# The last attention branch of a four-layer model: its input split in two halves, its first two weight chunks side by side, and gates by tanh

## The chip, the cores and the metric

The kernel runs on one core of one Trainium2 chip. The metric is device time in microseconds (us) of one execution of the whole program; lower is better.

## What is computed

Four transformer layers over 256 tokens of width 1024, in fp32. Layers 0 and 1 have a delta rule, a pooling and a retention as mixers; layers 2 and 3, which the change is mostly about, have three kinds of attention (`a` with a top-64 choice of keys, `b` dilated, `c` windowed with sinks). Each layer gates three branch products and sums them:

```python
g = jax.nn.sigmoid(gates.reshape(Bsz, L, N_BRANCHES, D_MODEL))
merged = (g[:, :, 0] * (o_a.reshape(Bsz, L, -1) @ w_a)
          + g[:, :, 1] * (o_b.reshape(Bsz, L, -1) @ w_b)
          + g[:, :, 2] * (o_c.reshape(Bsz, L, -1) @ w_c))
return merged @ w_o
```

`w_a` has 384 rows, `w_b` 256 and `w_c` 512; all have 1024 columns. After `w_o` comes a norm and a feed-forward block (`w_up`, squared relu, `w_down`). Layers 0 and 1 gate three branches in the same way.

## The kernel before

Everything is kept transposed: 128 features on the partitions, the 256 tokens along the free axis. A weight matrix comes as chunks of 128 x 1024 elements (eight 128 x 128 tiles, 512 KB) through four raw buffers. fp32 accuracy is made of two rounded parts: for each chunk ScalarE (ACT) copies `raw` to the high part `whi` and VectorE (DVE) makes the low part `wlo = raw - whi` (every second chunk or so of the second half is made by GpSimd, POOL, instead: `SHARED`, L155 on). Both go to rings of four buffers. An input of a product is split in the same way (`hh`/`hl`, `B0H`/`B0L`, `B2H`/`B2L`, `FH`/`FL`). Each tile of a product then is three matmuls (`mm3`, L1867), so a chunk is 24 matmuls on TensorE (PE).

All engines walk the same list of jobs, each in its own program order, and wait for each other by semaphores. While a chunk `i` is multiplied, ACT and DVE split chunk `i + 3` (`STAGED`); that split must wait until PE has used chunk `i - 1` up (the signal `used`). In layers 2 and 3 the attention's small steps are interleaved with a filler of weight products: `run(attention(...), fill)`, with the filler q2b (16 chunks), gate0 (8), gate1 (8), wa (3), gate2 (8), wb (2). The attention has ten rounds, numbered by `turn` 0 to 9; each round passes through five segments (scores, exponentials, turning the probabilities, values, output turned back to `OO`), and the rounds overlap. Rounds 6 to 9 are kind `c` and make wc's input, the four blocks 5 to 8 of `OO`: rounds 6 and 8 write blocks 5 and 6 for the first and the second half of the tokens, rounds 7 and 9 blocks 7 and 8. So the first half of wc's input is complete after round 8, the second after round 9. When the ten rounds are over, one filler step is left: the second chunk of wb. After that comes wc, then wo.

At the end of attention the program order is: ACT copies the output of round 9 to `OO`, makes `B2H` (`branch_high`, L780), then in the filler splits the chunk of wb's last step, and at wc's begin computes two sigmoids of 128 x 1024 in place (`branch`, L790). DVE makes `B2L` (`branch_low`, L1271), then splits a chunk, then evacuates the last two banks of wb: `evac` (L1282) multiplies a bank of two product tiles by the gate. The products of wb, wc, gate0 to gate2 alternate between two PSUM banks, 6 and 7; PE's `fresh` (L1856) waits until the previous contents of a bank were evacuated. POOL adds the gated products to `YY`. In wc, `merge` (L813 on ACT, L1302 on DVE) splits the sum `YY` to `FH` and `FL`, the input of wo, by quarters.

ScalarE's function tables: `act` (L614) loads the set `natural_log_exp_and_others` by hand ahead of an Exp or Ln when another function's set was in use last (L611 in the profile); ahead of a Sigmoid the load is put in by the compiler (L618). In the norm ahead of the feed-forward (`factor`, L652) an Ln and an Exp follow PE's sum, and the products of `up` can't be evacuated before them.

Of the kernel before, what the change touches and what calls it, by code (L numbers as in the profile page):

```python
# [25 lines left out]
EXPLN = "natural_log_exp_and_others"  # L26

# [173 lines left out]
def rest(steps):  # L201
    for _ in steps:
        pass
# [61 lines left out]
def program(nc, ins, out):  # L265
    with ExitStack() as ctx:
# [111 lines left out]
        BR2 = slot_r("B2H", 11, 4), slot_r("B2L", 13, 4)  # L378
# [226 lines left out]
        def scalar(a):  # L605
            table = [None]

            def ln_exp():
                if table[0] != EXPLN:
                    table[0] = EXPLN  # L610
                    a.preload_act_table_set(EXPLN)  # L611

            def act(dst, src, fn, scale=1.0, **more):
                if fn in (AF.Exp, AF.Ln):  # L614
                    ln_exp()
                elif fn in (AF.Silu, AF.Sigmoid, AF.Sin):
                    table[0] = str(fn)
                return a.activation(dst, src, fn, scale=scale, **more)  # L618
# [170 lines left out]

            def branch(name, L, merged=False):  # L790
                gate, dst = BRANCH[name][2:]

                def begin():
                    for j in (0, 2):
                        a.wait_ge(*v_evac.at(gate, L, 2 * j + 2))
                        d = dst[:, 512 * j:512 * j + 1024]
                        act(d, d, AF.Sigmoid).then_inc(*a_br.up("gate", name, L, j))

                begin()
# [13 lines left out]
            def merge(name, L, j):  # L813

                a.wait_ge(*gated(name, L, 2 * j))
                a.copy(FH[:, 2 * j:2 * j + 2, :], v3(pair(YY, j))).then_inc(*a_br.up("sum", L, j))
# [99 lines left out]
            def second(L):  # L916
# [29 lines left out]

                def index(half):
# [13 lines left out]
                def attend(x):  # L961
# [11 lines left out]
                    for q, (b, c0, heads) in enumerate(x.spread):  # L973
# [4 lines left out]
                        else:  # L978
                            p = a.copy(PT[:, c0:c0 + m], bank[b][:, 0:m])
                        p.then_inc(*a_att.up("PT", L, t, q))  # L980
                    yield
# [4 lines left out]

                fill = chain(project("q2b", L), project("gate0", L),
                             after_step(project("gate1", L), 5, lambda: branch_high("wa", L, *a_att.at("OO", L, 1))),
                             branch("wa", L),
                             after_step(project("gate2", L), 5, lambda: wb_high()),  # L990
                             branch("wb", L))
# [6 lines left out]
                branch_high("wc", L, *a_att.at("OO", L, 9))  # L998
                rest(fill)
                rest(branch("wc", L, merged=True))  # L1000

# [52 lines left out]
        def vector(v):  # L1054
# [224 lines left out]
            def branch(name, L, merged=False):  # L1279
                gate = BRANCH[name][3]  # L1280

                def evac(m0):  # L1282
# [4 lines left out]
                    if name in FIRST_BRANCH:  # L1287
                        tt(YY[:, c], b[:, :], gate[:, c], OP.mult).then_inc(*v_evac.up(name, L, m0))
                        return
                    tt(gate[:, c], b[:, :], gate[:, c], OP.mult).then_inc(*v_evac.up(name, L, m0))  # L1290
# [1284 lines left out]
```

## Time and profile before

| | us |
|---|---|
| median of 3 runs | 1928.36 (1928.3 to 1932.68) |
| the profiled execution, its own time | 1935.99 |
| span of its trace | 1934.2 |
| PE busy | 1887.0 (98% of the span) |
| DVE busy | 1238.2 (64%) |
| ACT busy | 958.4 (50%) |
| POOL busy | 311.4 (16%) |

A busy PE need not be at its peak, so the places are found by the idle time in front of an instruction and what ended it. Layers 2 and 3 repeat each other 449.5 us apart, and layer 2 is read except where said. Times in rows are us from the start of the span unless marked ns.

### The profile page before, as it was taken

How to read it: one execution, taken by the hardware profiler on the slowest of the kernel's cores; microseconds unless marked ns; L12 is line 12 of the kernel's file. 1: busy time of each engine (PE TensorE's matmuls, PEld its weight loads, DVE VectorE, ACT ScalarE, POOL GpSimd, SP SyncE). 2: the span in 40 equal slices, each digit the busy share in tenths (PEclk: the TensorE clock that was granted, in tenths of full speed). 3: DMA queues.
4: the chain of work that ended last, by engine and by line, in shares of the span. 5: the costliest groups of instructions: out<-in, count | busy, mean ns of one | idle time of the engine just before them, and what ended most of it. 6: DMA issues, size and time to landing. Idle time of an engine off the chain costs nothing.

```text
span 1934.2 us, 35101 instructions
## 1 busy us (share of the span) xinstructions
PE 1887.0 (98%) x14820; PEld 1800.6 (93%) x14820; DVE 1238.2 (64%) x1667; ACT 958.4 (50%) x1375; POOL 311.4 (16%) x174
## 2 busy tenths in 40 slices
PE   7999999999999999999999999999999999999998
PEld 7989998998889999999988999999999999999997
DVE  6884577665579545867657775577646684567743
ACT  5533365544563344654445445655534444656632
POOL 1050121000014102200001352310000353220000
PEclk9999999999999999999999999999999999999999
DMA  5443344656344323545665553345555763345652
GB/s 209 158 138 108 121 161 140 215 196 205 134 142 159 115 99 127 201 164 186 196 206 176 178 190 121 132 153 198 188 186 172 219 191 123 131 161 176 197 196 99
DMA packets 91580, 317.50 MB, mean 164 GB/s; under 512 B 11552, under 2 KB 12704, under 8 KB 91040
## 3 DMA queue, kind: packets, MB, share of 16 engines
q1 hardware_dynamic: 91424, 315.26, 48.7%
q8 instruction: 118, 1.93, 0.4%
q14 instruction: 38, 0.31, 0.0%
HBM read 304.99 MB, written 1.05 MB: 158 GB/s over the span
## 4 chain that ended last, share of the span: by engine, by line
PE 83%; DVE 12%; ACT 4%; issue 1%; DMA 0%; SPq 0%; ACTq 0%; DVEq 0%
PE bank L1863 81%; DVE wlo L1056 4%; DVE area L1056 3%; DVE area L1062 2%; ACT area L618 1%; ACT whi L624 1%; PE bank L2302 1%; PE bank L2042 1%; DVE xT L1062 0%; DMA raw<-in_weights 0%; DVE hl L1062 0%; DVE area L1527 0%; ACT hh L618 0%; DVE area L1525 0%; PE bank L2320 0%
## 5 line engine op out<-in xcount | busy, mean ns | idle before, releaser
L1056 DVE TENSOR_TENSOR wlo<-raw,whi 128x1024 fp32r<-128x1024 f32 x512 | 657.0, 1296 | 427.6 <-ACT whi L624 427.2
L1863 PE MATMUL bank<-hh,whi 128*128 128x256 f32 x2928 | 834.0, 285 | 26.4 <-DVE wlo L1056 18.7
L1863 PE MATMUL bank<-hl,whi 128*128 128x256 f32 x2928 | 817.6, 279 | 0.0
L1863 PE MATMUL bank<-hh,wlo 128*128 128x256 f32 x2928 | 817.4, 279 | 0.0
L624 ACT CAST whi<-raw 128x1024 fp32r<-128x1024 f32 x572 | 588.2, 1046 | 398.5 <-PE bank L1863 368.5
L1863 PEld LDWEIGHTS bank<-hh,whi 128*128 128x128 f32 x2928 | 556.9, 190 | 41.8 <-issue 15.1
L1863 PEld LDWEIGHTS bank<-hl,whi 128*128 128x128 f32 x2928 | 556.0, 190 | 1.5 <-issue 1.4
L1863 PEld LDWEIGHTS bank<-hh,wlo 128*128 128x128 f32 x2928 | 555.7, 190 | 0.0
L1655 POOL TENSOR_TENSOR area<-area 128x512 f32<-128x512 f32 (+4 forms) x90 | 138.3, 1544 | 929.8 <-ACT area L618 675.9
L1655 POOL TENSOR_TENSOR wlo<-raw,whi 128x1024 fp32r<-128x1024 f32 x60 | 151.5, 2526 | 332.1 <-ACT whi L624 331.7
L1863 PE MATMUL bank<-area 128*128 128x128 f32 (+5 forms) x1544 | 200.3, 289 | 4.1 <-DVE area L1056 3.3
L1863 PEld LDWEIGHTS bank<-area 128*128 128x128 f32 (+2 forms) x1544 | 181.2, 188 | 18.4 <-DVE area L1056 4.6
L1863 PE MATMUL bank<-FH,whi 128*128 128x256 f32 x640 | 178.6, 279 | 0.0
L1863 PE MATMUL bank<-FL,whi 128*128 128x256 f32 x640 | 178.3, 279 | 0.0
L1863 PE MATMUL bank<-FH,wlo 128*128 128x256 f32 x640 | 178.2, 279 | 0.0
L618 ACT ACTIVATE area<-area 128x256 f32<-128x256 f32 (+9 forms) x247 | 140.0, 578 | 60.3 <-DVE area L1056 20.7
L1056 DVE TENSOR_TENSOR area<-bank,area 128x512 f32<-128x512 f32 (+4 forms) x194 | 116.6, 629 | 57.1 <-PE bank L1863 52.9
L1863 PEld LDWEIGHTS bank<-FH,whi 128*128 128x128 f32 x640 | 121.5, 190 | 0.1
L1863 PEld LDWEIGHTS bank<-FL,whi 128*128 128x128 f32 x640 | 120.1, 188 | 0.1
L1863 PEld LDWEIGHTS bank<-FH,wlo 128*128 128x128 f32 x640 | 120.1, 188 | 0.0
L1056 DVE TENSOR_TENSOR area<-bank,RSB 128x512 f32<-128x512 f32 (+1 forms) x118 | 80.4, 682 | 51.4 <-PE bank L1863 51.4
L1863 PE MATMUL bank<-wlo,FH 128*128 128x512 f32 x240 | 94.6, 394 | 0.0
(123 smaller groups left out, 1883.6 us busy)
## 6 DMA issues: line engine op xcount, KB each, us to landing
raw<-in_weights SPq DMA_DIRECT2D x572, 512.0 KB, 3.7
area<-area SPq DMA_DIRECT2D x96, 64.0 KB, 3.7
area<-area SPq DMA_DIRECT2D x16, 128.0 KB, 3.8
cst<-in_const SPq DMA_DIRECT2D x1, 1188.0 KB, 10.1
cst<-in_const SPq DMA_DIRECT2D x1, 1024.5 KB, 5.6
xT<-in_x SPq DMA_DIRECT2D x4, 256.0 KB, 5.8
out<-xT SPq DMA_DIRECT2D x1, 1024.0 KB, 3.8
area<-in_lev SPq DMA_DIRECT2D x2, 384.0 KB, 7.7
```

Of the source, the lines that this page charges most:

```text
L618: return a.activation(dst, src, fn, scale=scale, **more)
L624: a.copy(whi[:, i % RING, :], raw[:, i % RAW, :]).then_inc(*hi.up(i))
L1056: return v.tensor_tensor(dst, x, y, op)
L1062: return v.scalar_tensor_tensor(out=dst, in0=x, scalar=s, in1=y, op0=op0, op1=op1)
L1655: return g.tensor_tensor(dst, x, y, op)
L1863: return e.matmul(ps, x, y, start=start, stop=stop, skip_group_check=skip)
L2042: x = e.transpose(bank[b0 + j][:, 128 * (b % 4):128 * (b % 4) + 128], block(src, b), C("eye"))
L2302: o = e.transpose(bank[b][:, 128 * u:128 * u + 128], x.grid()[:, j % 2, j // 2, 128 * kb:128 * kb + 128], C("eye"))
```

## The change

Chunks of wc are called F, F+1, F+2 and F+3; wo's are F+4 to F+11.

- `B2H` and `B2L` move from slots that the attention uses to its end to slots 3 and 4 (query and key blocks of kind `b`, free by then). Their 128 x 1024 split becomes two of 128 x 512: `wc_high(0)` and `wc_low(0)` in round 9's third segment, `wc_high(1)` and `wc_low(1)` after the attention.
- PE runs wc by `last_branch`: it waits for chunks F and F+1 and for both banks, multiplies the first half of the input with both chunks, then the second half, then F+2 and F+3 one after the other.
- Sigmoid(x) becomes (tanh(x/2) + 1)/2: ACT computes the tanh, DVE's `evac` adds 1 and multiplies (`scalar_tensor_tensor` in place of `tensor_tensor`), and `merge` multiplies by 0.5. This holds for all four layers.
- In layers 2 and 3 the set `exp_and_others` (Exp and Tanh) is loaded once ahead of attention and the logarithm's set after wc's merges; the gates are computed in the filler: wa's after steps 1 and 3 of gate1, wb's after steps 0 and 1 of wa, wc's after steps 0 and 1 of wb. As a step's follow-up runs when the filler is next called, wc's first gate stands after `wc_high(1)` and ahead of the split of chunk F+2, and its second behind that split.

```diff
-        BR2 = slot_r("B2H", 11, 4), slot_r("B2L", 13, 4)
+        BR2 = slot_r("B2H", 3, 4), slot_r("B2L", 4, 4)
@@ scalar
-                if fn in (AF.Exp, AF.Ln):
+                if fn is AF.Tanh:
+                    tables(EXPTANH)
+                elif fn is AF.Ln or fn is AF.Exp and table[0] != EXPTANH:
                     ln_exp()
...
+            def gate(name, L, j):
+                projection, dst = BRANCH[name][2:]
+                a.wait_ge(*v_evac.at(projection, L, 2 * j + 2))
+                d = dst[:, 512 * j:512 * j + 1024]
+                act(d, d, AF.Tanh, scale=0.5).then_inc(*a_br.up("gate", name, L, j))
...
-                a.copy(FH[:, 2 * j:2 * j + 2, :], v3(pair(YY, j))).then_inc(*a_br.up("sum", L, j))
+                act(FH[:, 2 * j:2 * j + 2, :], v3(pair(YY, j)), AF.Copy, scale=0.5).then_inc(*a_br.up("sum", L, j))
...
                 rest(project("v2b", L, v_second))
+                tables(EXPTANH)
+                def wc_high(j):
+                    a.wait_ge(*a_att.at("OO", L, 8 + j))
+                    a.copy(BR2[0][:, 2 * j:2 * j + 2, :], v3(BRANCH["wc"][1])[:, 2 * j:2 * j + 2, :]).then_inc(*a_br.up("high", "wc", L, j))
...
+                def gates(name, steps, *at):
+                    for i, s in enumerate(steps):
+                        yield s
+                        if i in at:
+                            gate(name, L, 2 * at.index(i))
                 fill = chain(project("q2b", L), project("gate0", L),
-                             after_step(project("gate1", L), 5, lambda: branch_high("wa", L, *a_att.at("OO", L, 1))),
-                             branch("wa", L),
+                             gates("wa", after_step(project("gate1", L), 5, lambda: branch_high("wa", L, *a_att.at("OO", L, 1))), 1, 3),
+                             gates("wb", branch("wa", L), 0, 1),
                              after_step(project("gate2", L), 5, lambda: wb_high()),
-                             branch("wb", L))
+                             gates("wc", branch("wb", L), 0, 1))
...
                 run(attention(index, attend), fill)
-                branch_high("wc", L, *a_att.at("OO", L, 9))
+                wc_high(1)
                 rest(fill)
                 rest(branch("wc", L, merged=True))
+                ln_exp()
@@ vector
-                    tt(gate[:, c], b[:, :], gate[:, c], OP.mult).then_inc(*v_evac.up(name, L, m0))
+                    stt(gate[:, c], gate[:, c], 1.0, b[:, :], OP.add, OP.mult).then_inc(*v_evac.up(name, L, m0))
...
-                tt(FL[:, 2 * j:2 * j + 2, :], v3(pair(YY, j)), FH[:, 2 * j:2 * j + 2, :].bitcast(F32), OP.subtract).then_inc(*v_br.up("merged", L, j))
+                stt(FL[:, 2 * j:2 * j + 2, :], v3(pair(YY, j)), 0.5, FH[:, 2 * j:2 * j + 2, :].bitcast(F32), OP.mult, OP.subtract).then_inc(*v_br.up("merged", L, j))
...
                 run(attention(index, attend), fill)
-                branch_low("wc", L)
+                wc_low(1)
@@ tensor
+            def last_branch(L):
+                job = JOBS["wc", L]
+                h, lo = BR2
+                for c in (0, 1):
+                    e.wait_ge(*wlo_at(job.first + c))
+                    fresh(job.banks[2 * c], leaves("wc", L, 2 * c))
+                for j in range(2):
+                    e.wait_ge(*v_br.at("low", "wc", L, j))
+                    for m in range(4):
+                        i, b = job.first + m // 2, job.banks[m // 2 * 2]
+                        for k in (2 * j, 2 * j + 1):
+                            x = mm3(bank[b][:, T * (m % 2):T * (m % 2) + T], i, 128 * (4 * (m % 2) + k), h[:, k, :], lo[:, k, :], (m % 2, k) == (0, 0), k == 3, True)
+                        if j and m % 2:
+                            x.then_inc(*proj.up("used", i, also=("wc", L, m - 1)))
+                for c in (2, 3):
+                    ...
-                rest(branch("wc", L))
+                last_branch(L)
```

## Rows read from the trace of the kernel before

**Rows 1.** PE's waits over the whole run: released by, total us, times, longest.
```profile
PE bank L1863 <- DVE wlo L1056: 18.7, 11, 11.3
PE bank L1863 <- DVE area L1056: 9.9, 9, 2.4
```
**Rows 2.** Timeline of PE, start, us, what [idle before]: wb's chunks and wc's begin.
```profile
1254.69 0.35 PE L1863 MATMUL bank<-B0H,whi 128*128 128x256 f32 x1 [0.30 <-DVE area L1056]
...
1260.09 0.35 PE L1863 MATMUL bank<-B2H,whi 128*128 128x256 f32 x1 [2.34 <-DVE area L1056]
```
**Rows 3.** Timeline of DVE over the same stretch and into wc.
```profile
1252.71 1.23 DVE L1056 TENSOR_TENSOR wlo<-raw,whi 128x1024 fp32r<-128x1024 f32 x1 [0.96 <-ACT whi L624]
...
1255.92 2.33 DVE L1056 TENSOR_TENSOR B2L<-area,B2H 128x1024 fp32r<-128x1024 f32 x1 [0.78 <-ACT B2H L788]
1258.17 1.21 DVE L1056 TENSOR_TENSOR wlo<-raw,whi 128x1024 fp32r<-128x1024 f32 x1
1259.31 1.27 DVE L1056 TENSOR_TENSOR area<-bank,area 128x512 f32<-128x512 f32 x2
...
1263.26 0.69 DVE L1056 TENSOR_TENSOR area<-bank,area 128x512 f32<-128x512 f32 x1 [0.23 <-PE bank L1863]
```
**Rows 4.** Timeline of ACT, end of attention and wo's weight splits.
```profile
1248.45 1.28 ACT L618 ACT_TABLE_LOAD   x1
...
1251.65 1.03 ACT L624 CAST whi<-raw 128x1024 fp32r<-128x1024 f32 x1
1254.43 0.37 ACT L984 COPY area<-bank 128x256 f32<-128x256 f32 x1 [1.74 <-PE bank L2320]
1254.83 1.06 ACT L788 CAST B2H<-area 128x1024 fp32r<-128x1024 f32 x1
1255.78 1.05 ACT L624 CAST whi<-raw 128x1024 fp32r<-128x1024 f32 x1
1256.74 2.00 ACT L618 ACTIVATE area<-area 128x1024 f32<-128x1024 f32 x2
...
1283.03 1.05 ACT L624 CAST whi<-raw 128x1024 fp32r<-128x1024 f32 x1 [1.78 <-PE bank L1863]
```
**Rows 5.** Timeline of POOL: the adds of wb's first two banks.
```profile
1254.62 2.54 POOL L1655 TENSOR_TENSOR area<-area 128x512 f32<-128x512 f32 x2 [3.73 <-DVE area L1056]
```
**Rows 6.** Layer 3: wc's begin on PE, its evacuation, the last merge, the split behind it.
```profile
1709.60 0.55 PE L1863 MATMUL bank<-B2H,whi 128*128 128x256 f32 x1 [2.44 <-DVE area L1056]
...
1714.19 0.69 DVE L1056 TENSOR_TENSOR area<-bank,area 128x512 f32<-128x512 f32 x1 [1.66 <-PE bank L1863]
...
1726.08 2.95 ACT L624 CAST whi<-raw 128x1024 fp32r<-128x1024 f32 x3
...
1727.16 1.23 DVE L1056 TENSOR_TENSOR wlo<-raw,whi 128x1024 fp32r<-128x1024 f32 x1 [0.26 <-ACT whi L624]
```
**Rows 7.** Windows: us, PE busy (matmuls), granted clock, DMA share, GB/s.
```profile
1709.40:1712.80 3.40, 3.20 (x15) 0.50 0.45 154
```
**Rows 8.** Timeline of ACT and PE: the norm ahead of the feed-forward's products.
```profile
1301.65 1.28 ACT L611 ACT_TABLE_LOAD   x1 [2.75 <-PE bank L1863]
1302.95 0.48 ACT L618 ACTIVATE RSB<-bank,cst 128x256 f32<-128x256 f32 x1
...
1307.58 0.38 PE L1863 MATMUL bank<-hh,whi 128*128 128x256 f32 x1 [0.50 <-DVE wlo L1056]
```
**Rows 9.** Timeline of ACT, then DVE, as attention begins.
```profile
1082.88 0.60 ACT L618 ACTIVATE area<-bank 128x512 f32<-128x512 f32 x1 [0.29 <-PE bank L1863]
...
1094.93 1.29 DVE L1056 TENSOR_TENSOR area<-bank,area 128x512 f32<-128x512 f32 x2 [0.94 <-PE bank L1863]
```
**Rows 10.** Groups by form: count, busy us, mean ns, idle before.
```profile
L1056 DVE TENSOR_TENSOR area<-bank,area 128x512 f32<-128x512 f32 x156 | 102.1, 683 | 22.9 <-PE bank L1863 19.1 <-PE bank L2042 3.4
L1062 DVE SCALAR_TENSOR_TENSOR area<-bank,area 128x512 f32<-128x512 f32 x4 | 2.6, 680 | 0.0
L788 ACT CAST B0H<-area 128x512 fp32r<-128x512 f32 x2 | 1.2, 608 | 0.0
```

More of the change, by code:

```diff
@@ L606, in scalar, with tables @@
             table = [None]
+            def tables(which):
+                if table[0] != which:
+                    table[0] = which
+                    a.preload_act_table_set(which)
             def ln_exp():
-                if table[0] != EXPLN:
-                    table[0] = EXPLN
-                    a.preload_act_table_set(EXPLN)
+                tables(EXPLN)
             def act(dst, src, fn, scale=1.0, **more):
-                if fn in (AF.Exp, AF.Ln):
+                if fn is AF.Tanh:
+                    tables(EXPTANH)
+                elif fn is AF.Ln or fn is AF.Exp and table[0] != EXPTANH:
                     ln_exp()
-                elif fn in (AF.Silu, AF.Sigmoid, AF.Sin):
+                elif fn in (AF.Silu, AF.Sin):
                     table[0] = str(fn)
@@ L788, in branch_high @@
                 a.copy(BRANCH[name][0][0][:, 0:nk, :].rearrange("p k t -> p (k t)"), BRANCH[name][1]).then_inc(*a_br.up("high", name, L))
-            def branch(name, L, merged=False):
[L791 to L799, printed above, removed]
+            def gate(name, L, j):
[3 more added lines that the diff above has]
+                act(d, d, AF.Tanh, scale=0.5).then_inc(*a_br.up("gate", name, L, j))
+            def branch(name, L, merged=False):
+                if L < DEPTH:
+                    gate(name, L, 0)
+                    gate(name, L, 2)
                 if not merged:
@@ L980, in attend @@
                         p.then_inc(*a_att.up("PT", L, t, q))
+                    if t == 9:
+                        wc_high(0)
                     yield
@@ L1287, in evac @@
                     if name in FIRST_BRANCH:
[L1288 removed]
+                        stt(YY[:, c], gate[:, c], 1.0, b[:, :], OP.add, OP.mult).then_inc(*v_evac.up(name, L, m0))
                         return
[L1290 removed]
+                    stt(gate[:, c], gate[:, c], 1.0, b[:, :], OP.add, OP.mult).then_inc(*v_evac.up(name, L, m0))
                     if m0 == 6:
@@ L1569, in attend @@
                     v.reciprocal(x.den, x.den).then_inc(*v_att.up("den", L, t))
+                    if t == 9:
+                        wc_low(0)
                     yield
@@ L1580, in attend, with wc_low @@
                     yield
+                def wc_low(j):
+                    v.wait_ge(*a_br.at("high", "wc", L, j))
+                    at = slice(2 * j, 2 * j + 2)
+                    tt(BR2[1][:, at, :], v3(BRANCH["wc"][1])[:, at, :], BR2[0][:, at, :].bitcast(F32), OP.subtract).then_inc(*v_br.up("low", "wc", L, j))
                 def gate2(m0):
@@ L2216, in branch @@
                 yield from project(name, L, h, lo, lambda j: v_br.at("low", name, L))
+            def last_branch(L):
[13 more added lines that the diff above has]
+                for c in (2, 3):
+                    i, b = job.first + c, job.banks[2 * c]
+                    e.wait_ge(*wlo_at(i))
+                    fresh(b, leaves("wc", L, 2 * c))
+                    for m in range(2):
+                        for k in range(4):
+                            x = mm3(bank[b][:, T * m:T * m + T], i, 128 * (4 * m + k), h[:, k, :], lo[:, k, :], k == 0, k == 3)
+                    x.then_inc(*proj.up("used", i, also=("wc", L, 2 * c)))
             def first(L):
```

1 line of the change is left out of this document (added).

## The prediction

> **What bounds the kernel now.** TensorE (PE) is busy for 98% of the span, so time is won or lost only where PE stands still or runs slower. I read PE's waits of the whole run first [rows 1]: the long ones are for weight splits early in the run and for VectorE's (DVE) results; 9.9 us in nine waits, the longest 2.4, are for DVE's work on `area`. Two of those nine are the places that the change aims at. The timeline shows the place in layer 2 [rows 2]: PE waits 0.30 us ahead of wb's second chunk, finishes it at 1257.75 (that is 1260.09 less 2.34) and begins wc at 1260.09. Layer 3 has the same picture, 2.44 us long [rows 6]. A third stop follows in the norm ahead of `up`, 0.50 us [rows 8]; I take the same in layer 3. If all of it went, 2 x (0.30 + 0.50) + 2.34 + 2.44 = 6.4 us would be won, 0.33% of the run. That is the ceiling of what waits are worth here.
>
> Then I asked which chain ends the 2.3 us. `B2H` begins 0.03 us after ACT's last output copy (1254.43 + 0.37 = 1254.80) and takes 1.06 [rows 4]; `B2L` takes 2.33, since it runs beside POOL's two adds [rows 3, 5]. But PE doesn't begin when `B2L` is there (1258.25). DVE next splits the chunk F+2 (1.21 us), and only then evacuates wb's last two banks, 1259.31 on, 0.60 from one to the next; PE's 1260.09 is the end of the first of these (1260.00) plus 0.09 [rows 2, 3]. So the wait ends with a bank that DVE frees behind two other works in its queue. The split F+2 in turn can't start before ACT's copy of F+2, 1255.78 to 1256.83 [rows 4], which is early today and hidden behind `B2L`.
>
> **The change, part by part.** (1) The first half of `B2H`/`B2L`. Round 8's output is copied a round earlier, and ACT gets 3.2 us free, as the load and two sigmoids leave (the load starts at 1248.45, and the next split at 1251.65 [rows 4]). A 128 x 512 copy costs 0.61 on ACT [rows 10] and DVE's half half of 1.22, the time of an undisturbed 128 x 1024 split [rows 3]; both are covered by PE's chunk of gate2. Cost nothing. If that cover were gone they would cost 1.2 us a layer.
>
> (2) wb's second chunk. The load and the sigmoids (3.2 us) leave ACT ahead of the split F+1, so DVE does this split before 1252.7 and not from 1252.71 on [rows 3, 4], and frees wb's first bank as soon as PE has filled it. PE's 0.30 goes; wb ends at 1257.45.
>
> (3) The start of wc, the main term. What is late next? ACT, counted by the distance from one start to the next [rows 4]: output copy ends 1254.80; `wc_high(1)` starts 1254.83 and, at half of 0.95, gives way at 1255.35 (0.52, with the fixed part); the new first gate, a tanh of 128 x 1024, which I price as the sigmoid (2.00 for two, so about 0.95 a piece), 1256.30; the split of F+2 ends 1.05 later, 1257.35. `wc_low(1)` is done by then, even if it waits for POOL's adds to end: those follow wb's evacuations and end at about 1256.1. DVE splits F+2 from 1257.38 (1.14 to the next start), evacuates the first bank from 1258.52 and the second from 1259.12 to 1259.80. And `last_branch` waits for both banks before its first matmul, not for one as now. PE begins at 1259.80 + 0.09 = 1259.89, against 1260.09: 0.20 us won of 2.3. The gate that was moved ahead of the split takes what the halved split gives. Bounds: nothing (the tanh longer by 0.2) to 2.64 (the wait goes wholly); the chain of rows is complete, so I stay at 0.20.
>
> (4) Side by side. Work on PE is the same 96 matmuls, 2.83 us a chunk (ACT's split of 1283.03 sits 1.05 long with 1.78 idle before it, paced by PE [rows 4]). But the first chunk is given back after 36 matmuls and not 24: 4.25 us after wc's start, plus the 0.34 that lies between that and DVE's evacuation today (1263.26 - 1260.09 - 2.83). Layer 3 shows by chance what that does downstream: there its first chunk ran at a half clock, and DVE's evacuation began 1714.19 - 1709.60 = 4.59 us after wc's start [rows 6]. So I read the rest of the branch there. No stall of PE followed within wc. The split of wo's fourth chunk, F+7, started on DVE at 17.56 after wc's start, behind all four merges. PE will want that chunk (4 + 3) x 2.83 = 19.81 after the start. Today it has 1.0 us to spare.
>
> (5) The tables. In layers 2 and 3 four loads (1.28 each) become two. The one that leaves the norm is on the path: PE's sum, load, Ln, Exp, DVE, split, PE [rows 8]; the chain gets 1.28 shorter and PE's 0.50 goes, no more. The one that is put behind the merges stands on ACT ahead of the split of F+7: 17.56 + 1.28 + 1.23 = 20.07, plus 0.09 is 20.16, so PE stops 0.35 us. Bounds of that: zero, to 1.44 if one more collision with POOL (2.33 - 1.22 = 1.1 [rows 3]) gets into the chain of merges. I take 0.35, the row's. The load as attention begins delays two small works by about half a us [rows 9]; DVE has 0.94 idle further down before PE needs it. Nothing. Loads and sigmoids inside attention: PE doesn't wait there, nothing.
>
> (6) DVE's adds of 1 and the scalings: `scalar_tensor_tensor` with a bank takes 0.680, `tensor_tensor` 0.683 [rows 10]. Nothing, in all four layers. In layers 0 and 1 the number of loads stays, as a logarithm follows.
>
> The Trainium skill ("ScalarE: Activation LUTs", What ACT_TABLE_LOAD costs) says that a switch costs a drain of about 1380 ns beside the 1283 ns of the load. The trace speaks against a visible drain: the Ln begins 1.30 us after the load's start [rows 8]. By the page's figure the stop in wo would be an estimated 1.7 us and the sum 2.1 us slower; I go by the row.
>
> **Sum.** Per layer -0.20 + 0.35 - 0.50 = -0.35, so -0.7 for both. The profiled execution would go from 1935.99 (span 1934.2 and 1.8 around it) to 1935.3. It is 7.6 above the median of the runs, and none of the terms depends on what lies between them, so I carry the difference over: 1928.36 - 0.7 = 1927.7.
>
> **The rivals.** *The clock.* In layer 3 the granted clock fell to 0.50 (1.2 GHz) right where the idle stretch ended, for 3.4 us [rows 7]; the first evacuation came 4.59 - 3.17 = 1.42 us later than in layer 2. In layer 2 a wait 0.1 shorter had no such fall. After the change PE's idle stretch is 2.44 (1257.45 to 1259.89), and 2.54 in layer 3: as long as now. So the fall may go (1927.7 - 1.4 = 1926.3), stay, or come in both layers (1929.1). Nothing in the rows tells which; 18% and 17%.
>
> *The gap closes wholly.* If PE found both banks free and the halves ready, layer 2 would win 2.64 + 0.50 - 0.35 = 2.8, layer 3 2.9 and its 1.42 of clock: 7.1, so 1921.3. For it: the low half is what the wait seems to be for. Against it: the bank is, and ACT's order. 6%.
>
> *wo's fourth chunk comes late (slower).* The place is PE's fourth chunk of wo; the mechanism is the ring: chunks given back 1.4 us later, merges behind them, the table load behind these, then the split. It decides from the point where DVE ends that split later than 19.8 us after wc's start. At 1.44 a layer: -0.20 + 1.44 - 0.50 = +0.74, twice 1.5: 1929.9. For it: only 1.0 us to spare with 1.28 put in. Against: layer 3's rows have most of it in already. 8%.
>
> *The change doesn't do what it says.* If the set with Exp doesn't serve the tanh (or the reverse), the compiler puts loads in again, one of 1.28 in ACT's chain of (3): +1.28 a layer, 1928.36 - 0.7 + 2.6 = 1930.2. For: Sigmoid needed its own load at L618 until now. Against: Ln and Exp share one. 5%.
>
> **How the numbers follow.** Forecast 46%, clock gone 18%, clock in both 17%, late chunk 8%, gap closed 6%, loads 5%. The likeliest is 1927.7. The range 1924.0 to 1931.0 leaves out the closed gap and a late chunk or loads that meet the clock, and holds a part-closed gap. About 0.3%, 5.8 us, is what a measurement of this kernel can tell from no change: below 1922.6 lies the closed gap (6%), above 1934.1 only mishaps that add up (3%).
>
> **What would show it.** Right: in the trace of after PE's wait ahead of wc is 2.3 to 2.7 us and ends with DVE's second evacuation of wb; the split of F+2 starts on ACT at about 1.5 us after the output copy's end, behind a tanh; the 0.30 and the 0.50 are gone; a short stop appears at wo's fourth chunk, released by `wlo`. Wrong: a wait ahead of wc under 1 us; a stop inside wc (a bank not freed by its second evacuation); any load between Exp and tanh; new waits of PE within attention.

## The result and the profile after

| | before | after |
|---|---|---|
| median, us (20 runs of each, taken together) | 1934.42 (1926.9 to 1938.17) | 1938.9 (1930.4 to 1948.5) |
| profiled execution, us (its span) | 1935.99 (1934.2) | 1942.33 (1940.5) |
| ratio, with its 95% interval | | 1.0029 [1.0016, 1.0042] |

The forecast was 1927.7, with 1924.0 to 1931.0: that is 0.7 us faster. The kernel became slower by 4.5 us (difference of the medians) to 5.6 (the ratio). So the sign was wrong, though the size is just under the 0.3% that I called "same". Some 6 us of the distance between 1927.7 and 1938.9 are no effect of the change: the kernel before itself came out at 1934.42 here, against 1928.36 in its three first runs. That fact turned out to be a clue. One profiled execution, that of bank_and_order_2, ran at a granted clock of 0.85 from end to end (2083.5 us, where its series otherwise lies between 1920.52 and 1941.04), and neither its time nor its trace is used.

The page of after, busy time of each engine:
```profile
PE 1891.2 (97%) x14820; PEld 1804.8 (93%) x14820; DVE 1245.0 (64%) x1669; ACT 952.8 (49%) x1373; POOL 307.8 (16%) x174
```
PE's waits over the whole run of after, released by, total us, times, longest; to be laid beside [rows 1]:
```profile
PE bank L1895 <- DVE wlo L1080: 18.6, 11, 11.3
PE bank L1895 <- DVE area L1080: 6.2, 6, 1.9
PE bank L1895 <- DVE area L1086: 5.9, 2, 2.9
```
The timeline of PE in after: a matmul ahead of wb's second chunk, wc's first, and wo's fourth chunk, in layer 2; then the last two places in layer 3.
```profile
1254.91 0.28 PE L1895 MATMUL bank<-B0H,wlo 128*128 128x256 f32 x1
...
1261.43 0.35 PE L1895 MATMUL bank<-B2H,whi 128*128 128x256 f32 x1 [2.93 <-DVE area L1086]
...
1283.27 0.36 PE L1895 MATMUL bank<-FH,whi 128*128 128x256 f32 x1 [0.75 <-DVE wlo L1080]
...
1715.01 0.36 PE L1895 MATMUL bank<-B2H,whi 128*128 128x256 f32 x1 [2.93 <-DVE area L1086]
...
1736.85 0.36 PE L1895 MATMUL bank<-FH,whi 128*128 128x256 f32 x1 [0.34 <-DVE wlo L1080]
```
Against [rows 2, 6 and 8]: the 0.30 ahead of wb's second chunk is gone (no bracket around 1254.91), so is the norm's 0.50; the wait ahead of wc is 2.93 in both layers instead of 2.34 and 2.44; and wo's fourth chunk has a stop of its own. Below I count a stop from the start of the last matmul before it to the first one behind it, where two matmuls without a stop lie 0.12 apart.

ACT and DVE of after as wb ends, and as wo begins (to be laid beside [rows 3 and 4]):
```profile
1255.80 0.37 ACT L1000 COPY area<-bank 128x256 f32<-128x256 f32 x1 [3.73 <-PE bank L2376]
1256.20 0.62 ACT L959 CAST B2H<-area 128x512 fp32r<-128x512 f32 x1
1256.73 1.06 ACT L624 ACTIVATE area<-area 128x1024 f32<-128x1024 f32 x1
1257.69 1.03 ACT L630 CAST whi<-raw 128x1024 fp32r<-128x1024 f32 x1
...
1279.51 1.28 ACT L612 ACT_TABLE_LOAD   x1
1280.81 3.90 ACT L630 CAST whi<-raw 128x1024 fp32r<-128x1024 f32 x4
```
```profile
1256.86 1.34 DVE L1080 TENSOR_TENSOR B2L<-area,B2H 128x512 fp32r<-128x512 f32 x1 [0.59 <-ACT B2H L959]
1258.76 1.23 DVE L1080 TENSOR_TENSOR wlo<-raw,whi 128x1024 fp32r<-128x1024 f32 x1 [0.56 <-ACT whi L630]
1259.90 1.28 DVE L1086 SCALAR_TENSOR_TENSOR area<-area,bank 128x512 f32<-128x512 f32 x2
...
1281.89 4.63 DVE L1080 TENSOR_TENSOR wlo<-raw,whi 128x1024 fp32r<-128x1024 f32 x4 [1.68 <-ACT whi L630]
```
Windows of PE behind wc's start in after: us, PE busy (matmuls), granted clock, DMA share, GB/s:
```profile
1262.40:1265.70 3.30, 3.30 (x17) 0.50 0.37 129
1716.40:1719.70 3.30, 3.30 (x18) 0.50 0.41 146
```
Before, only layer 3 had such a stretch at 0.50 (1.2 GHz) [rows 7]; in after both layers have it.

**What these places add up to.** wb's stop and the start of wc together: the output copy begins at 1255.80 and wc 5.63 later, against 5.66 before (1260.09 - 1254.43): nothing. The norm's two stops, 0.77 and 0.78, are 0.12 now: -1.3. wo's fourth chunk, 1.02 and 0.61 instead of 0.12: +1.4. One more stretch at half clock: +1.4. The sum is +1.5. The two profiled executions differ by 6.3. Another 1.6 is one stop in layer 3, as attention begins, which the second trace of the same kernel (below) doesn't have:
```profile
1583.14 0.36 PE L1895 MATMUL bank<-hh,whi 128*128 128x256 f32 x1 [1.45 <-DVE area L1080]
```
That leaves 3.2 us without a stop of that size, and 2.4 of them lie between matmuls that don't wait at all.

### The profile page after: what moved, and what is told of

Its sections match the earlier page's. It is cut to its first block, busy times and chain, and to the rows that moved or that the text cites. A ratio compares the mean times of both kernels' runs of the same rounds, so it can differ in the third digit from the quotient of the medians.

```text
span 1940.5 us, 35101 instructions
## 1 busy us (share of the span) xinstructions
PE 1891.2 (97%) x14820; PEld 1804.8 (93%) x14820; DVE 1245.0 (64%) x1669; ACT 952.8 (49%) x1373; POOL 307.8 (16%) x174
## 4 chain that ended last, share of the span: by engine, by line
PE 82%; DVE 13%; ACT 4%; issue 2%; DMA 0%; SPq 0%; DVEq 0%; ACTq 0%
PE bank L1895 80%; DVE wlo L1080 5%; DVE area L1080 3%; DVE area L1086 2%; ACT area L624 2%; ACT whi L630 1%; PE bank L2358 1%; PE bank L2074 1%; DVE xT L1086 0%; DVE area L1551 0%; DVE area L1549 0%; DVE area L1083 0%; DVE hl L1086 0%; DMA raw<-in_weights 0%; ACT hh L624 0%
## 5 line engine op out<-in xcount | busy, mean ns | idle before, releaser
L624 ACT ACTIVATE area<-area 128x256 f32<-128x256 f32 (+8 forms) x247 | 140.7, 579 | 61.0 <-DVE area L1080 21.0
L1080 DVE TENSOR_TENSOR area<-bank,area 128x512 f32<-128x512 f32 (+4 forms) x146 | 84.1, 610 | 44.9 <-PE bank L1895 41.2
```

The lines of the kernel that those rows point to most:

```text
L1080: return v.tensor_tensor(dst, x, y, op)
```

## PE runs at one of two paces

I laid the 14,820 matmuls of both traces side by side, by number. Away from stops, at full granted clock, the distance between two matmuls of 128 x 256 isn't one number. It is 113.3 ns or 117.8 ns, hardly anything between, and it holds for hundreds of matmuls, in the long stretches for more than a thousand. In the 19 traces at full clock that this study has, it never changes within 96 or more matmuls that follow each other without a break. The kernel after passes from one to the other inside the norm of layer 2; its PE timeline there, wo's last matmuls, the sum with ones, then `up`:
```profile
1302.10 0.28 PE L1895 MATMUL bank<-hl,whi 128*128 128x256 f32 x1
1302.22 0.28 PE L1895 MATMUL bank<-hh,wlo 128*128 128x256 f32 x1
1302.33 0.28 PE L1895 MATMUL bank<-hh,whi 128*128 128x256 f32 x1
1302.44 0.28 PE L1895 MATMUL bank<-hl,whi 128*128 128x256 f32 x1
1302.56 0.28 PE L1895 MATMUL bank<-hh,wlo 128*128 128x256 f32 x1
1302.67 1.89 PE L1895 MATMUL bank<-area,cst 128*128 128x256 f32 x8
1304.21 0.47 PE L1895 MATMUL bank<-hh,whi 128*128 128x256 f32 x1
1304.51 0.28 PE L1895 MATMUL bank<-hl,whi 128*128 128x256 f32 x1
1304.63 0.28 PE L1895 MATMUL bank<-hh,wlo 128*128 128x256 f32 x1
1304.75 0.28 PE L1895 MATMUL bank<-hh,whi 128*128 128x256 f32 x1
1304.87 0.28 PE L1895 MATMUL bank<-hl,whi 128*128 128x256 f32 x1
1304.99 0.28 PE L1895 MATMUL bank<-hh,wlo 128*128 128x256 f32 x1
```
Four steps take 0.46 us above (1302.10 to 1302.56) and 0.48 below (1304.51 to 1304.99). A window of 50 us holds about 443 matmuls at the short distance and 427 at the long one. The same two windows, first in layer 2 and then in layer 3, for before and then for after and for a second profile of the same kernel (after_again); columns as above:
```profile
1380.00:1430.00 50.00, 50.00 (x427) 1.00 0.57 190
1830.00:1880.00 50.00, 50.00 (x443) 1.00 0.59 198
```
```profile
1380.00:1430.00 50.00, 50.00 (x427) 1.00 0.59 187
1830.00:1880.00 50.00, 50.00 (x444) 1.00 0.64 197
```
```profile
1380.00:1430.00 50.00, 50.00 (x427) 1.00 0.60 190
1830.00:1880.00 50.00, 50.00 (x427) 1.00 0.60 189
```
PE is busy all the time and the clock is 1.00 in all six: the page's share of busy time can't show this, only the count can. One kernel has it either way in different executions. The some 1450 matmuls of `up` and `down` behind a norm take 1450 x 4.5 ns = 6.5 us more at the long distance, over four times what all the places add up to. The first traces of before and after have the same pace in both windows, so the 2.4 us of pace between those two lie outside `up` and `down`. The same program's executions spread over 11 us here (1926.9 to 1938.17; over all series of the kernel before 1926.54 to 1950.82), and in the traces that follow the pace goes a long way with that: the three with the short pace in both layers have spans of 1923.6 to 1932.0, the eight with the long one in both 1933.2 to 1942.7. It isn't all: before_again, with the paces of before in both windows, has a span 4.7 us shorter, and about 5 us less of stops and half clock in layers 0 and 1.

## The experiments

Ratios are to the kernel before, run beside it on the same chip, 12 runs of each experiment; the brackets are 95% intervals. First the kernel after once more, and three undoings. "The rest" below is the mean difference to before minus what stops and half-clock stretches in the trace give; I work it out for all kernels further down.

**after_again.** Nothing edited.

> The changed kernel as it is, to learn what repeats. Theory 'places' (the loss sits where PE stops: 2.93 us ahead of wc in both layers, a clock at 1.2 GHz behind it, 0.9 and 0.5 us at wo's fourth chunk, 1.45 us as attention begins in layer 3): these stops stand at the same instructions again, and the ratio to the kernel before is 1.002 to 1.004. Rival 'pace' (in the two traces PE needs either 2.72 or 2.83 us for 24 matmuls without any wait, and the stretches of either differ; that makes 2.8 of the 6.3 us between the traces): the stretches lie elsewhere in this trace, though the kernel is the same, and the stop as attention begins in layer 3 may be gone.

1.0031 [1.0008, 1.0053], 1941.84 us. Same stops (3.21 at wc in both layers, 1.02 at wo in both), the half clock in one layer only, and the long pace in both layers. The slowdown is real, and which stretches are at which pace changes from one execution to the next. In the profile of after the 1.45 us stop as attention begins in layer 3 looked like an effect of the change; it isn't here, so it was chance. A stop of that length comes elsewhere too, in layer 2 of before_no_stop_3 (1.73 us between starts), a kernel without the change.

**no_side.** The last branch in the project order, chunk by chunk.
```diff
-                last_branch(L)
+                h, lo = BR2
+                rest(project("wc", L, h, lo, lambda j: v_br.at("low", "wc", L, j)))
```


> The changed kernel, with wc's chunks one after the other on PE as before (the input still split in halves, one bank waited for). Theory 'the second bank and the two chunks held': PE begins wc after the first evacuation, 0.6 us sooner, and gives the first chunk back 1.4 us sooner, so the stop at wo's fourth chunk goes (0.9 and 0.5 us): 1.3 us a layer, 2 to 3 us in all against the changed kernel. Rival 'ACT's order alone': the wait ahead of wc stays above 2.2 us and the clock still falls behind it, so under 1.5 us is won.

1.0023 [1.0001, 1.0045]. wc's wait is 2.45 (both layers), and wo's fourth chunk isn't stopped any more:
```profile
1262.95 0.36 PE L1895 MATMUL bank<-B2H,whi 128*128 128x256 f32 x1 [2.18 <-issue]
```
So waiting for both banks, which went together with the order of the chunks, costs 3.21 - 2.45 = 0.76 a layer, and giving the first chunk back late is needed for wo's stop. At the places it is 3.5 us better than after in all (the half clock came once), and the time gives 2.4 of them back only by the means (+5.2 against +2.8), with a rest of +4.8.

**gate_behind.** The two gates of wc go behind the splits on ACT.
```diff
-                             gates("wc", branch("wb", L), 0, 1))
+                             branch("wb", L))
...
                 rest(fill)
+                gate("wc", L, 0)
+                gate("wc", L, 2)
```


> The changed kernel, with wc's first tanh on ACT behind the split of chunk F+2 (both gates after the last step of wb). Theory 'the tanh holds the split up': the wait ahead of wc shrinks from 2.93 to 2.0 us in both layers, and with it the fall of the clock may go (1.5 us in each): 2 to 5 us faster than the changed kernel. Rival 'low half and POOL': DVE's second half then ends at 1.4 us behind ACT's high half and the wait shrinks by 0.4 us or less.

1.0016 [0.9998, 1.0034]. The tanh ahead of the split of F+2 was worth 3.21 - 2.56 = 0.65 us of wait:
```profile
1259.37 0.36 PE L1897 MATMUL bank<-B2H,whi 128*128 128x256 f32 x1 [2.28 <-DVE area L1088]
```
That carries the prediction's reading of ACT's order. No half clock followed in either layer.

**loads_idle.** Both table loads go where ACT has slack: tanh's two steps earlier in v2b, the logarithm's into wo's fifth step.
```diff
-                rest(project("v2b", L, v_second))
-
-                tables(EXPTANH)
+                rest(after_step(project("v2b", L, v_second), 1, lambda: tables(EXPTANH)))
...
                 rest(branch("wc", L, merged=True))
-                ln_exp()
...
-                by_rows("wo", L)
+                by_rows("wo", L, {5: ln_exp})
```


> The changed kernel, with both table loads put where ACT idles for PE: the one with tanh after the second chunk of v2b, the logarithm's after wo's sixth split. Theory 'loads on DVE's chain': attention's begin loses its shift (ACT's first relu 1.4 us after PE's start as in the kernel before), the stop of 1.45 us in layer 3 goes, and wo's fourth chunk waits 0.2 us or nothing: 1.5 to 3.5 us faster than the changed kernel. Rival 'the loads are covered': within 0.8 us of it.

1.0036 [1.0012, 1.0059], no better than after. Its wc wait is as in after (3.20, a bracket of 2.93), the half clock came in both layers, in layer 2 for twice as long as elsewhere (26 matmuls in the 5.6 us from 1258.0); wo's fourth chunk and the norm don't stop. With ln_in_norm below, which takes away that load alone, it shows that the load behind the merges makes wo's stop; and without that stop the times are no better.

**before_again.** Nothing edited in the kernel before.

> The kernel before, unchanged, for a second trace. Theory 'places': 2.6 and 2.7 us between starts at wc, 0.57 ahead of wb's second chunk, 0.78 in both norms, as in the first trace. Theory 'pace': the stretches with 2.72 and 2.83 us for a chunk lie elsewhere than in the first trace of the same program, and the long stretch of up and down (64 chunks) costs 6.8 us more at the one than at the other; the two compared series, of one program, lie within 1.002 of each other.

1.0008 [0.9987, 1.0029]. Same stops as before, no half clock, paces 427 and 443 in a span of 1929.5.

**ln_in_norm.** The kernel after, with the logarithm's load back in the norm.
```diff
                 rest(branch("wc", L, merged=True))
-                ln_exp()
```


> The changed kernel, with the logarithm's table loaded in the norm again, as before. Theory 'the load behind the merges stops PE in wo': the stop at wo's fourth chunk (1.02 us between starts in three of four places) falls to 0.3 or nothing, and the norm's stop of 0.78 is back in both layers: net 0.4 us faster than the changed kernel at the places. Rival 'the two chunks held do it alone': 0.6 us or more are left at wo's fourth chunk.

0.9992 [0.9972, 1.0011]: this one line takes 5.6 us back by the means (+5.2 to -0.4), though its places add up to +0.4, against after's +1.5. No stop at wo, a stop of 0.57 at the norm in both layers, long pace in layer 2, short in layer 3:
```profile
1380.00:1430.00 50.00, 50.00 (x427) 1.00 0.58 191
1830.00:1880.00 50.00, 50.00 (x444) 1.00 0.60 197
```

**bank_and_order.** loads_idle, and the three causes of wc's wait taken away: the gates early on ACT, DVE evacuates wb's last banks before it splits F+2, and PE waits bank by bank.
```diff
+                def wb_and_gates():
+                    for i, s in enumerate(branch("wb", L)):
+                        if i == 0:
+                            gate("wc", L, 0)
+                            gate("wc", L, 2)
+                        yield s
...
+                    last = name == "wb" and chunks[0] == JOBS[name, L].first + 1
+                    if last:
+                        for m0 in done:
+                            evac(m0)
...
-                        if evac:
+                        if evac and not last:
...
-                for c in (0, 1):
-                    e.wait_ge(*wlo_at(job.first + c))
-                    fresh(job.banks[2 * c], leaves("wc", L, 2 * c))
...
+                        if not j and m % 2 == 0:
+                            c = m // 2
+                            e.wait_ge(*wlo_at(job.first + c))
+                            fresh(job.banks[2 * c], leaves("wc", L, 2 * c))
```


> The changed kernel with five repairs, two chunks side by side kept: both gates of wc on ACT between wb's first split and the last output copy; DVE evacuates wb's last two banks ahead of the split of F+2; PE waits for a bank only when it comes to it; both table loads where ACT idles. Theory 'DVE's queue and ACT's gate make the wait': PE's wait ahead of wc falls from 3.2 to under 0.6 us between starts in both layers, no clock fall there, no stop in wo: 2 x (2.6 + 0.9) = 7 us of stops less than the changed kernel, about 2 x 2.9 less than the kernel before, and the ratio to before is 0.996 to 0.999. Rival 'pace decides': the stops go, but the time stays within 0.1% of the kernel before, because slow stretches take it back.

```profile
1257.40 0.36 PE L1903 MATMUL bank<-B2H,whi 128*128 128x256 f32 x1 [0.44 <-DVE area L1090]
```
The mechanism of the wait is shown: 0.71 instead of 3.21 (expected: under 0.6), the clock stays at 1.00, nothing stops at wo or at the norm. That is 6.9 us better than before at the places, and the ratio is 0.9994 [0.9971, 1.0017]: outside the 0.996 to 0.999 of the theory, and within the 0.1% of before that the rival 'pace decides' had. Nearly 5 us are missing.

**order_one_by_one.** The same repairs in project's order, against bank_and_order:
```diff
-                last_branch(L)
+                h, lo = BR2
+                rest(project("wc", L, h, lo, lambda j: v_br.at("low", "wc", L, j)))
```

> The same repairs, with wc's chunks one after the other. Theory: the wait ahead of wc ends with the second low half (1.4 us after ACT's high half of it), since the first chunk's third tile needs it: 0.3 to 1.2 us between starts somewhere in wc's first chunk, 0.5 us a layer behind the kernel with side by side. Rival 'side by side is worth nothing': the same stops in both.

0.9989 [0.9966, 1.0011], wait 0.67. With the bank and the queues put right, side by side brings nothing measurable.

By now every kernel without a stop in layer 3's norm that I had profiled had the long pace behind it, except the first profile of after; every one with it had the short one. The next runs ask whether that stop matters.

**before_no_stop.** The kernel before, with the load behind the merges, which takes the norm's stop away.
```diff
                 rest(branch("wc", L, merged=True))
+                ln_exp()
```


> The kernel before, with one line more: the logarithm's table is loaded right behind wc's merges in layers 2 and 3 and not in the norm. Nothing else of the change. Theory 'redrawn pace' (the short stop in the norm sets PE's pace for the 60 chunks of up and down that follow: 2.72 us a chunk in layer 3 in all three traces that have the stop, 2.83 in six of seven that haven't): the stop of 0.78 us is gone and layer 3's up and down run at 2.83, so this kernel is 2 to 5 us SLOWER than before (6.5 us where the pace turns, less 1.3 for both stops, less what layer 2 may gain). Rival 'places': 1.3 us faster, 0.9993.

> The kernel before with the logarithm's load behind the merges, once more. Its first trace had layer 3's up and down at 2.83 us a chunk, but its series was not slower than before (0.9992). Theory 'redrawn pace': the pace is 2.83 again in this trace, and the two series together are 1 us or more slower than before. Rival 'the pace without the stop is open': 2.72 in this trace or the next, and the time within 1 us of before, or faster by the 1.3 us of the two stops.

> The same kernel a third time, same expectations: theory 2.83 us a chunk in layer 3 and slower than before; rival 2.72 in one of them and no loss.

Three series: 0.9992 [0.9967, 1.0018], 0.9998 [0.9980, 1.0015], 1.0010 [0.9990, 1.0030]. The traces have layer 3 long, short, long. The second one shows that the stop isn't necessary for the short pace; its windows, in a span of 1925.9 us:
```profile
1380.00:1430.00 50.00, 50.00 (x443) 1.00 0.62 198
1830.00:1880.00 50.00, 50.00 (x444) 1.00 0.61 200
```
In time, the theory had 2 to 5 us slower than before and the rival 1.3 us faster. The mean of the three is +0.5, some 1.2 us uncertain, with a rest of +2.0: it lies between the two and decides for neither, and the second trace is what the rival had said.

**after_with_stop.** The kernel after with a needless load once the norm's sum is there, all else kept.
```diff
+                def norm_factor():
+                    a.wait_ge(*e_norm.at("sum", f"mlp{L}"))
+                    a.preload_act_table_set(EXPLN)
+                    factor(f"mlp{L}")
...
-                rest(project("up", L, mlp, lambda: factor(f"mlp{L}")))
+                rest(project("up", L, mlp, norm_factor))
```


> The changed kernel, with a second and needless load of the logarithm's table in the norm, so that only the stop there comes back. Theory 'redrawn pace': layer 3's up and down go to 2.72 us a chunk, and the kernel is 3 to 5 us faster than the changed one (ratio to before about 1.0005), though it does more. Rival 'places': 0.9 to 1.3 us slower than the changed kernel, 1.0035.

1.0005 [0.9981, 1.0028]. It has the stops of after and the norm's two more, and in layer 2 the half clock lasted twice as long (26 matmuls in the 5.5 us from 1260.0), so +4.4 at the places, and is 3.8 us faster than after by the mean (+1.4 against +5.2). The norm's stop on PE, and the windows behind it:
```profile
1310.58 0.38 PE L1900 MATMUL bank<-hh,whi 128*128 128x256 f32 x1 [0.50 <-DVE wlo L1085]
...
1380.00:1430.00 50.00, 50.00 (x427) 1.00 0.58 189
1830.00:1880.00 50.00, 50.00 (x444) 1.00 0.61 195
```

**repairs_stop.** bank_and_order's repairs, but the logarithm's load left in the norm (no `ln_exp` anywhere else); **repairs_two_loads** has after_with_stop's load (its diff above) besides. Against bank_and_order:
```diff
-                by_rows("wo", L, {5: ln_exp})
+                by_rows("wo", L)
```

> The kernel with the repairs and side by side (PE's wait ahead of wc 0.71 us), with the logarithm's table in the norm again. Theory 'redrawn pace': both gains together, layer 3 at 2.72 us a chunk and 5 us fewer stops and clock falls than before: 0.996 to 0.9985. Rival 'places': 1 us slower than the repaired kernel without the stop, 0.9998.

> The same with two loads in the norm one after the other, so that PE's stop there is 1.28 us longer, about 1.9 to 2.0 us. Theory 'any stop redraws, its length doesn't matter': layer 3 stays at 2.72 and layer 2 at 2.83, and it is 2.6 us slower than with one load. Rival 'the stop's length picks the pace': the pace of at least one layer turns, 6.5 us up or down.

> The repaired kernel with the logarithm's table in the norm, a second series (first 0.9954). Theory: stops 2.0 us shorter in each layer at wc, none in wo, no clock fall at wc, layer 3 at 2.72: 0.995 to 0.998 again. Rival 'the first series was lucky': above 0.998.

repairs_stop: 0.9954 [0.9931, 0.9976] and, in a second series, 0.9969 [0.9944, 0.9993], with medians of 1927.47 and 1929.33. It is the fastest kernel of the study, faster than before and than after. The wait at wc, layer 2:
```profile
1258.24 0.36 PE L1903 MATMUL bank<-B2H,whi 128*128 128x256 f32 x1 [0.44 <-DVE area L1090]
```
Its first trace has the short pace in both layers and a span of 1923.6, its second has the long one in both and 1937.8, the one exception among the kernels with the stop:
```profile
1380.00:1430.00 50.00, 50.00 (x443) 1.00 0.64 199
1830.00:1880.00 50.00, 50.00 (x443) 1.00 0.64 198
```
```profile
1380.00:1430.00 50.00, 50.00 (x427) 1.00 0.57 190
1830.00:1880.00 50.00, 50.00 (x427) 1.00 0.57 189
```
repairs_two_loads stops 1.86 in each norm instead of 0.57, and still has 0.9965 [0.9942, 0.9989], with the short pace in both layers: a longer stop costs its length and gives no more.

**after_third** and **bank_and_order_2.** Nothing edited, for a second or third trace and series.

> The changed kernel a third time. Places (certain by now): 3.21 us between starts at wc twice, a stop at wo's fourth chunk, none in the norm. Theory 'redrawn pace': layer 3 at 2.83 us a chunk (first trace 2.72, second 2.83), ratio 1.002 to 1.004. Rival: 2.72 at the same ratio, so that the loss would lie elsewhere.

> The repaired kernel without the stop in the norm, a second series on one chip with the next kernel. Theory 'redrawn pace': layer 3 at 2.83 us a chunk, and 3 to 6 us slower than the repaired kernels with the stop (0.998 to 1.000 against before). Rival 'places': 1.2 us faster than those, 0.9955.

after_third: 1.0020 [1.0000, 1.0039], long pace in both layers. bank_and_order_2: 0.9982 [0.9955, 1.0008]; its trace isn't read. Its ratio lies within the theory's 0.998 to 1.000, and the interval just reaches the rival's 0.9955.

**repairs_stop_layer_3.** repairs_stop, with the norm's stop in layer 3 only.
```diff
-                by_rows("wo", L)
+                by_rows("wo", L, {5: ln_exp} if L == 2 else {})
```


> The repaired kernel with the logarithm's load in the norm of layer 3 only; in layer 2 it stands in ACT's idle time in wo. Theory: layer 3 at 2.72 us a chunk as in six of seven traces with the stop, layer 2 without its stop of 0.6 us: 0.995 to 0.998. Rival 'chance': 2.83 in layer 3, 0.9985 to 1.000.

0.9980 [0.9950, 1.0010]. The trace is as expected (no stop and the long pace in layer 2, 0.57 and the short pace in layer 3), the time only partly: it lies between repairs_stop and bank_and_order, but with a rest of +2.8.

**All kernels in one table.** Places: stops and half-clock stretches of the traces, against the mean of before's two traces, us, a half-clock stretch at 1.4 and the two twice as long ones at 2.8. Measured: difference of the means, over 11 to 44 runs of each; its standard error is 1.2 to 2 us for a single series of 12 and 2.5 for bank_and_order_2. Rest: measured less places.

| kernel | norm's stops | places | measured | rest |
|---|---|---|---|---|
| after | none | +1.5 | +5.2 | +3.7 |
| no_side | none | -2.0 | +2.8 | +4.8 |
| gate_behind | none | -2.3 | +2.8 | +5.1 |
| loads_idle | none | +2.3 | +7.5 | +5.2 |
| bank_and_order | none | -6.9 | -2.2 | +4.7 |
| bank_and_order_2 | none | -6.9 | -4.9 | +2.0 |
| order_one_by_one | none | -7.0 | -1.7 | +5.3 |
| before_no_stop | none | -1.5 | +0.5 | +2.0 |
| repairs_stop_layer_3 | layer 3 | -6.5 | -3.7 | +2.8 |
| before_again | both | 0 | +2.1 | +2.1 |
| ln_in_norm | both | +0.4 | -0.4 | -0.8 |
| after_with_stop | both | +4.4 | +1.4 | -3.0 |
| repairs_stop | both | -5.9 | -8.5 | -2.5 |
| repairs_two_loads | both | -3.4 | -6.1 | -2.6 |

(bank_and_order_2 has the places of bank_and_order.) All eight rows without the stops in both layers have a rest of +2 or more, four of the five with both lie below zero. Layer 3's pace in the traces: short in 7 of 8 with a stop in its norm, in 2 of 11 without. Luck alone gives such a split in fewer than 1 of 100 cases, but I had the idea from ten of these traces, which split 3 of 3 and 1 of 7; the nine later ones split 4 of 5 and 1 of 4, which luck alone gives in one case of six. 6.5 us x (7/8 - 2/11) = 4.5 us is what this would make; the mean rests of the two halves of the table, +4.1 and -1.4, lie 5.5 apart. In layer 2 no such link is seen (short in 2 of 7 with, 3 of 12 without).

## Why the prediction was wrong, step by step

(1), the halves: right. The first ones in layer 2 took 0.63 on ACT (forecast 0.61) and 0.69 on DVE (half of 1.22), and PE waited for neither:
```profile
1248.74 0.63 ACT L959 CAST B2H<-area 128x512 fp32r<-128x512 f32 x1
1249.40 0.69 DVE L1080 TENSOR_TENSOR B2L<-area,B2H 128x512 fp32r<-128x512 f32 x1 [3.46 <-ACT B2H L959]
```
The second low half took 1.34, beside POOL's adds, and was done before DVE's next split could start.

(2), wb's 0.30: right, gone in every kernel with the load out of ACT's way.

(3), the start of wc: right in mechanism, and almost in every duration. From the output copy's start the first tanh begins 0.93 later (forecast 0.92), F+2's split 1.89 (1.87), DVE's split 2.96 (2.95), the evacuations 4.10 (4.09), the second ends 5.38 (5.37). Only PE's start was mis-sized, 0.25 behind that end and not 0.09: I had taken the 0.09 from a first evacuation's end, where two share a row. The term measured 0 in place of -0.20. no_side and gate_behind show two of the three causes that the step names, both banks (0.76) and the tanh (0.65). DVE's order was changed only together with them, in bank_and_order and its kin, where the wait fell by 2.50; what it is worth alone no run tells.

(4), side by side: right, no stop within wc. Its late return of the first chunk shows up at wo.

(5), the tables: the norm's stops went, loads went from four to two a layer, and a stop came at wo's fourth chunk, released by `wlo` behind the load, as said. It was sized 0.35 and measured 0.90 and 0.49 above the normal step, within the bounds of 0 to 1.44. The pace explains part: in all ten places with this stop (five traces) it is 1.02 from start to start where PE ran at 113.3 ns ahead of it, and 0.60 where it ran at 117.8, since a quicker PE wants the chunk sooner while ACT and DVE deliver it at the same moment: in the four of the ten without a half clock in wc, PE went on 20.20 to 20.34 us behind wc's start at either pace, where the forecast had 20.16. Of the Trainium skill's 1380 ns drain ("ScalarE: Activation LUTs", What ACT_TABLE_LOAD costs) nothing is seen again: the split starts 1.30 behind the load's start (1279.51 to 1280.81).

(6), DVE's forms: right, 1.28 for two, against 1.27 [rows 3].

**The rival of the clock** came: the chances of 18% gone and 17% both had the direction open. Over ten places with the wait of the kernel before, 2.6 to 2.7 us, the half clock followed twice; over four with 2.45 or 2.56 (no_side, gate_behind) once; over twelve with a wait of 3.2 us, nine times; in the repaired kernels with 0.7, never. Nine of the eleven behind the long waits of 2.6 us and more cost about 1.4 us, the two twice as long ones 2.8. I had called the idle stretch "as long as now", 2.44 against 2.34; it was 2.93. wb's end came 2.70 behind the start of the output copy (1261.43 - 2.93 - 1255.80) and not 3.02 (1257.45 - 1254.43), and wc began 5.63 behind it and not 5.46. So wb ends earlier than before and wc doesn't begin earlier: 3.21 from start to start, against 2.62. A gain ahead of a fixed end is paid into the wait. From 0.4 such stretches in an execution (two in ten places) to 1.33 (four in three traces of after) at 1.4 us each is 1.3 us that the sum should have held.

**The step that failed** is the sum's: "none of the terms depends on what lies between them". With all terms re-sized the places give +1.5, not the +5 measured. The rest isn't at the places; what the traces show there is the pace of PE, with layer 3 at the long one in two of after's three traces and in none of before's two. The prediction took 2.83 us a chunk as PE's constant [rows 4] and the norm's stop as 0.50 us of pure loss [rows 8]. The traces show that the distance of matmuls can change at such breaks and only there, and that without the norm's stop the long one more often follows in layer 3: ln_in_norm and after_with_stop put the stop back into the kernel after and win 4 to 6 us; repairs_stop is 4 to 6 faster than bank_and_order, with 1 us more of stops. The same step failed a second time where the difference was carried over onto 1928.36, a median of three runs: over 20 runs the kernel before has 1934.42, and 0.7 less than that, 1933.7, lies above the range already.

**What stays open.** What sets the pace. With before_no_stop, the one edit on the kernel before, neither side was decided. The stop isn't sufficient (repairs_stop_2) nor necessary (before_no_stop_2), layer 2 doesn't follow it, and repairs_stop_layer_3's time bears it out only weakly. Every kernel with the stop also has a table load in the norm, so the runs can't tell the two apart, nor the stop itself from where it leaves the other engines and the DMAs. That a load with its stop in the norm is worth more time than it costs is shown, for after and for the repaired kernel; that it does so by the pace is supported by counts in one trace per series, and its mechanism isn't known.

## What to carry to other kernels

A gain that ends earlier in front of a wait whose end stays lengthens the wait, and the longer wait was followed by half clock more often here (9 of 12 against 2 of 10): move the release (here a bank behind two works in DVE's queue), not the work ahead of it. Before a change of under 0.5% is forecast from one trace, count PE's matmuls per stretch at full clock in several executions; where that count changes, stops of half a us are the smaller matter. And a wait that is taken away isn't won until the stretch behind it has been compared too.

## What the hardware showed that I had not expected

Two paces of PE at the same granted clock of 1.00 and without any wait: 113.3 ns and 117.8 ns per matmul of 128 x 256 with its weight load, 443 and 427 matmuls in 50 us. The formula of the Trainium skill ("TensorE: Matmul & The Clock Gate", Back-to-back issue gap), there for a matmul by itself, would give an estimated 256 / 2.4 + 2.5 = 109 ns, and the page says that weight loads enter the spacing; neither pace is that figure, and the page has no second one. The pace holds over more than a thousand matmuls and changes only at breaks; DMA traffic in the windows is the same for a given pace (186 to 192 GB/s at the long one, 193 to 200 at the short one), as it would be if it only followed the rate at which PE uses up weights. All four combinations of layers 2 and 3 occur.
